# Modulation of a two-part sequence model: the weighted sum over input features is taken by VectorE, TensorE sums over partitions for three chunks at a time

## The chip, the cores and the metric

The kernel runs on one core of one Trainium2 chip. The metric is device time in microseconds of one execution of the whole program. Lower is better.

## The reference, cut to what matters

Two blocks of two layers each run one after the other on a sequence of 256 tokens with 1024 features. The first block mixes attention and a long convolution; its layers project the normed input with one wide matrix `w_in`. The second block's four sublayers are modulated by a vector that depends only on the conditioning input `c` (one row of 1024), not on the tokens:

```
def adaln(c, w, b):
    m = jax.nn.silu(c.astype(jnp.float32)) @ w + b
    shift, scale, gate = jnp.split(m, 3, axis=-1)
    return shift[:, None, :], scale[:, None, :], gate[:, None, :]
```

There are four such products, each of a 1 x 1024 row with a 1024 x 3072 matrix: 12288 outputs, each a sum over 1024 inputs. Since nothing but `c` goes in, the kernel computes all four while the first block runs. Everything is float32.

## The kernel before, in words

**Layout.** The four matrices are cut into 24 chunks of 512 output columns, 12 chunks for each layer `l` (0, 1) of the first block. A chunk is 2 MB: 128 partitions, and on each 8 slices of 512 numbers (input feature = slice k and partition). The projection weights of a layer are 16 chunks of the same size, named HV, Q, K_, V, HX1, HX2, ZA, ZH, GA0, GA1, GH0, GH1, PA, PH, WO0, WO1 (0 to 15).

**Loads.** `LOADS` is the order of the loads of a layer: w0 to w3, then m0, w4, m1, w5, ... m11, w15, where w is a projection chunk and m a modulation chunk. They go into a ring of four slots of `arena`. SyncE's queue (L406) issues them strictly in that order: load n waits until load n-4, which had the slot, is used up. `LOAD_END` says which TensorE group that is.

**Groups.** The program of a layer is the list `STEPS`, written out by hand in `layer_steps()`; every engine goes through it in order and does its share of each step. "proj" steps are TensorE groups of matmuls (two for each chunk up to GH1, four for PA and PH; WO0 and WO1 alternate for two token tiles). In this text g0 to g35 are the proj groups of a layer in order: chunk c has g2c and g2c+1 up to c = 11, PA is g24 to g27, PH g28 to g31, WO g32 to g35. Between the groups stand the attention and convolution steps of `after`: scores, mix (softmax weights), weigh, values, dft, idft, heads_out, heads_turn and so on.

**Two banks.** All groups, modulation groups too, write PSUM banks 0 and 1 in turn: group number `n` (`GROUP`, which numbers proj and modmul steps together) takes bank `n % 2`, and TensorE waits before it on `free[n % 2]`, that is until group n-2 has been drained. Q, K_, V, ZA to GH1 are drained by ScalarE, HX1, HX2, PA, PH by VectorE, WO by both.

**Modulation.** Before the first group of each chunk c from 4 on stands ("modmul", c-4): eight matmuls with 32 stationary columns (L592) on the eight slices of the chunk. `band` holds silu(c), one column of eight slices, with zeros around it, so that only row m of 32 gets chunk m's result, and the four column groups of the array each take two slices. ScalarE copies the bank out (L1272), and GpSimd adds it to `modsum` (L2311). Near the end of a layer ("mod", L599) turns the sums with four small matmuls.

**Chains.** On VectorE `link(ins)` lets the next instruction wait for this one.

## Time and profile before

| what | value |
|---|---|
| median of 3 runs | 1980.88 us (1980.46 to 1988.24) |
| span of the profiled execution | 1980.0 us |
| TensorE matmul busy in it | 1919.8 us, 97% |
| VectorE, ScalarE, GpSimd busy | 689.7, 372.2, 115.0 us |
| first block's layers in that profile | about 13.5 to 311 us, and 315 to 611 us |

The profiled execution has no time of its own beside its span on the page; the span lies 0.9 us under the median, so a difference read from the trace is a difference of the median. Times of rows are microseconds from the start of the span. In the groups of rows PE is TensorE's matmuls, DVE is VectorE, ACT ScalarE, POOL GpSimd, SPq SyncE's queue. One float32 matmul of the program shows as two matmuls in the profile.

### The profile page before, as it was taken

The numbers are of one execution on the slowest core, as the hardware profiler recorded it, in microseconds if no ns is written. First come the engines' busy times: TensorE is split into PE (matmuls) and PEld (weight loads), VectorE is DVE, ScalarE is ACT, GpSimd is POOL, SyncE is SP. The second block draws the span as 40 slices with busy tenths as digits, with TensorE's granted clock in tenths as the row PEclk, the third lists the DMA queues.
The fourth block names the chain that finished last, engine by engine and source line by source line (L and its number), as shares of the span: only waits on it lengthen the run. The fifth ranks groups of instructions, "written<-read, shape, count | busy, mean of one in ns | idle before, by whom it ended". The sixth has DMA issues, their size and how long they took to land.

```text
span 1980.0 us, 28488 instructions
## 1 busy us (share of the span) xinstructions
PE 1919.8 (97%) x11940; PEld 1070.5 (54%) x11940; DVE 689.7 (35%) x1472; ACT 372.2 (19%) x776; POOL 115.0 (6%) x98
## 2 busy tenths in 40 slices
PE   7999999999998999999989988999999999999998
PEld 6577866577865765776756544232323233333332
DVE  3364414354413573434449943010101010101112
ACT  3322102222103232234320012010101010101011
POOL 0000010000010000000016620000000000000000
PEclk9999999999999999999999998999999999999999
DMA  9255574264673316533323135999989999999993
GB/s 359 94 218 208 222 296 170 95 245 182 243 290 128 128 43 246 191 159 128 127 106 126 45 149 202 365 378 376 374 374 375 374 369 382 366 379 364 389 368 143
DMA packets 44037, 483.98 MB, mean 244 GB/s; under 512 B 5108, under 2 KB 6772, under 8 KB 10328
## 3 DMA queue, kind: packets, MB, share of 16 engines
q1 hardware_dynamic: 39136, 471.73, 59.2%
q10 hardware_dynamic: 4248, 9.07, 1.3%
q0 software_dynamic: 576, 2.10, 0.3%
q8 instruction: 55, 0.90, 0.2%
q14 instruction: 22, 0.18, 0.0%
HBM read 479.07 MB, written 10.10 MB: 247 GB/s over the span
## 4 chain that ended last, share of the span: by engine, by line
PE 88%; DVE 6%; DMA 3%; issue 1%; ACT 1%; ACTq 1%; POOL 0%; DVEq 0%; SPq 0%
PE bank L921 20%; PE bank L579 14%; PE bank L951 12%; PE bank L874 8%; PE bank L886 4%; PE bank L738 3%; PE bank L571 3%; PE bank L564 3%; PE bank L744 3%; PE bank L592 2%; PE bank L1000 2%; DMA arena<-bias_rows 1%; PE bank L1095 1%; PE bank L560 1%; PE bank L1028 1%; PE bank L935 1%
## 5 line engine op out<-in xcount | busy, mean ns | idle before, releaser
L921 PE MATMUL bank<-arena 128*32 128x512 f32 x4096 | 457.3, 592 | 0.0
L579 PE MATMUL bank<-arena 128*128 128x256 f32 x1408 | 313.3, 382 | 0.0
L921 PEld LDWEIGHTS bank<-arena 128*32 128x32 f32 x4096 | 136.1, 110 | 300.3 <-issue 300.3
L579 PEld LDWEIGHTS bank<-arena 128*128 128x128 f32 x1408 | 265.5, 190 | 54.2 <-issue 15.8
L951 PE MATMUL bank<-arena 128*32 128x512 f32 x2112 | 238.2, 595 | 0.0
L2077 DVE TENSOR_TENSOR arena<-arena,bank 128x256 f32<-128x256 f32 x64 | 27.0, 421 | 562.1 <-ACT arena L1447 511.6
L874 PE MATMUL bank<-arena 128*128 128x256 f32 x704 | 153.7, 379 | 0.1
L874 PEld LDWEIGHTS bank<-arena 128*128 128x128 f32 x704 | 133.6, 190 | 21.8 <-issue 4.1
L951 PEld LDWEIGHTS bank<-arena 128*32 128x32 f32 x2112 | 62.9, 109 | 133.3 <-issue 132.7
L1447 ACT ACTIVATE arena<-bank 128x256 f32<-128x256 f32 x64 | 24.6, 385 | 517.5 <-PE bank L921 517.4
L2323 POOL TENSOR_TENSOR arena<-arena 128x512 f32<-128x512 f32 x64 | 81.3, 1270 | 293.4 <-DVE arena L2131 290.9
L886 PE MATMUL bank<-arena 128*128 128x512 f32 x176 | 77.2, 592 | 0.0
L564 PE MATMUL bank<-arena 128*128 128x512 f32 x128 | 56.4, 596 | 1.8 <-ACT arena L1272 1.8
L738 PE MATMUL bank<-arena 128*128 128x256 f32 x256 | 56.8, 381 | 0.0
L744 PE MATMUL bank<-arena 128*128 128x512 f32 x128 | 56.4, 596 | 0.2 <-DVE arena L1966 0.2
L571 PE MATMUL bank<-arena 128*128 128x256 f32 x256 | 56.3, 381 | 0.0
L886 PEld LDWEIGHTS bank<-arena 128*128 128x128 f32 x176 | 33.4, 190 | 37.8 <-issue 37.3
L571 PEld LDWEIGHTS bank<-arena 128*128 128x128 f32 x256 | 48.3, 190 | 9.8 <-issue 3.4
L738 PEld LDWEIGHTS bank<-arena 128*128 128x128 f32 x256 | 48.2, 190 | 7.6 <-issue 0.8
L2052 DVE TENSOR_TENSOR arena<-arena,bank 128x256 f32<-128x256 f32 x22 | 9.3, 421 | 117.0 <-ACT arena L1422 116.9
L2311 POOL TENSOR_TENSOR arena<-arena 128x512 f32<-128x512 f32 x22 | 27.9, 1269 | 352.9 <-ACT arena L1272 352.9
L2334 POOL DMA_INDIRECT arena<-slot_rows,itab x4 | 4.0, 991 | 746.4 <-DVE itab L2214 745.5
(446 smaller groups left out, 1894.4 us busy)
## 6 DMA issues: line engine op xcount, KB each, us to landing
arena<-in_wgu SPq DMA_DIRECT2D x88, 2048.0 KB, 10.2
arena<-in_w SPq DMA_DIRECT2D x46, 2048.0 KB, 8.1
arena<-in_wdn SPq DMA_DIRECT2D x88, 1024.0 KB, 9.6
arena<-in_modw SPq DMA_DIRECT2D x24, 2048.0 KB, 9.3
arena<-in_wf SPq DMA_DIRECT2D x11, 3072.0 KB, 10.4
arena<-in_flt_deltas ACTq DMA_DIRECT2D x2, 1024.0 KB, 11.7
slot_rows<-arena ACTq DMA_DIRECT2D x7, 192.0 KB, 3.5
cst<-in_consts SPq DMA_DIRECT2D x1, 1162.0 KB, 7.7
```

What stands on the lines that cost most here:

```text
L564: ins = mm(bank[b][:, :], mT[:, k, h * P:(h + 1) * P], w[:, k * 512:(k + 1) * 512], start=(k == 0), stop=(k == KT - 1))
L571: ins = mm(bank[b][:, j * S:(j + 1) * S], w[:, col:col + P], y_in[:, k, :], start=(k == 0), stop=(k == 3))
L579: ins = mm(bank[b][:, j * S:(j + 1) * S], w[:, col:col + P], hT[:, k, :], start=(k == 0), stop=(k == KT - 1))
L592: ins = mm(bank[n % 2][r, :], band[:, k, 31 - c:63 - c], ring[at % RING][:, k * 512:(k + 1) * 512], start=(k < 4), stop=(k >= 4), skip_gro ...
L738: ins = mm(bank[n % 2][:, j * S:(j + 1) * S], w[:, col:col + P], hT[:, k, :], start=(k == 0), stop=(k == KT - 1))
L744: ins = mm(bank[n % 2][:, :], lhs(k), w[:, k * 512:(k + 1) * 512], start=(k == 0), stop=(k == KT - 1))
L874: ins = mm(bank[4 + f][:, u * S:(u + 1) * S], w[:, col:col + P], hT[:, k, :], start=(k == 0), stop=(k == KT - 1))
L886: ins = mm(bank[2 * t + i][:, :], hid[:, d % 2, f, t * P:t * P + P], w[:, col:col + 512], start=(d == 0 and f == 0), stop=(d == FFC - 1 an ...
L921: ins = mm(bank[w % 2][32 * j:32 * j + 32, :], hTe[:, k, TOK * b:TOK * b + TOK], wslot[SLOT[c]][:, k, :], start=(k == 0), stop=(k == KT - ...
L951: return mm(bank[4 + n][32 * g:32 * g + 32, :], lhs, dslot[c % RING][:, f, n * 512:(n + 1) * 512], start=first, stop=last, skip_group_chec ...
L1000: ins = mm(bank[6 + j // 4][:, (j % 4) * SLOTS:(j % 4 + 1) * SLOTS], xn[:, t, j * P:(j + 1) * P], oneh[:, t, 64:64 + SLOTS], start=(t == 0 ...
L2323: ins = pool.tensor_tensor(cz[o % 4][:, n], zz[:, o % 2], tab[o][:, n, :].unsqueeze(1).broadcast_to([P, 2, S]), ALU.mult)
```

## The change

The eight slices of a modulation chunk are no longer multiplied on TensorE. VectorE forms sum over k of silu(c)[k, p] * w[p, k, :] in SBUF: one tensor_scalar and seven scalar_tensor_tensor of 128 x 512 for each chunk, in two halves of four instructions (`modulation(l, m, part)`), each half put ahead of VectorE's share of a certain projection group (`MOD_SCALE`). TensorE sums the 128 partitions of three such sums in one group of four 32-column matmuls (one column group for each chunk, a fourth with zero weights), so a layer has four modmul groups in place of twelve: before g13, g22, g26 and g34 (`MOD_AT`). VectorE, not ScalarE, drains these banks and adds them to `modsum`; GpSimd does nothing for it any more. A modulation chunk's ring slot is given up when VectorE has ended its second half (`mod_sum`), not when TensorE has.

```diff
-GROUPS_1 = 36 + MOD_CHUNKS
+MOD_SETS = 4
+MOD_OF = MOD_CHUNKS // MOD_SETS
+MOD_AT = {13: 0, 22: 1, 26: 2, 34: 3}
+GROUPS_1 = 36 + MOD_SETS
+MOD_SCALE = {("proj", m + 3 + (1 + p) // 2, (1 + p) % 2): (m, p) for m in range(9) for p in range(2)}
+MOD_SCALE.update({("proj", PA, 2): (9, 0), ("proj", PA, 3): (9, 1), ("proj", PH, 0): (10, 0), ("proj", PH, 1): (10, 1), ("proj", WO0, 0): (11, 0), ("proj", WO1, 0): (11, 1)})
...
-                    sp.wait_ge(sm["grp_ps"], l * GROUPS_1 + LOAD_END[n - RING])
+                    if LOADS[n - RING][0] == "w":
+                        sp.wait_ge(sm["grp_ps"], l * GROUPS_1 + LOAD_END[n - RING])
+                    else:
+                        sp.wait_ge(sm["mod_sum"], l * MOD_CHUNKS + LOAD_END[n - RING])
...
                         pe.wait_ge(free[n % 2], l * (GROUPS_1 // 2) + n // 2)
-                        if c == 0:
-                            pe.wait_ge(sm["c_ready"], 1)
-                        pe.wait_ge(landed[at % RING], l * (16 * LOADS_1 // RING) + 16 * (at // RING + 1))
-                        for k in range(KT):
-                            r = slice(32 * (k % 4), 32 * (k % 4) + 32)
-                            ins = mm(bank[n % 2][r, :], band[:, k, 31 - c:63 - c], ring[at % RING][:, k * 512:(k + 1) * 512],
-                                     start=(k < 4), stop=(k >= 4), skip_group_check=True)
+                        pe.wait_ge(sm["mod_sum"], l * MOD_CHUNKS + MOD_OF * (c + 1))
+                        for q in range(4):
+                            m = MOD_OF * c + min(q, MOD_OF - 1)
+                            col = C_BAND + (31 - m if q < MOD_OF else 32)
+                            ins = mm(bank[n % 2][32 * q:32 * q + 32, :], cst[:, col:col + 32], mod_sums[m],
+                                     start=True, stop=True, skip_group_check=True)
...
+                            act.wait_ge(sm["grp_ps"], l * GROUPS_1 + GROUP[("modmul", 2, 0)] + 1)
...
-                        F(modout[:, c % 2, :], bank[n % 2][:, :], ACT.Copy).then_inc(free[n % 2], 1)
...
+            def modulation(l, m, part):
+                at = PLACE[("m", m)]
+                if part == 0:
+                    dve.wait_ge(landed[at % RING], l * (16 * LOADS_1 // RING) + 16 * (at // RING + 1))
...
+                w = ring[at % RING].rearrange("p (k n) -> p k n", k=KT)
+                for k in range(4 * part, 4 * part + 4):
+                    if k == 0:
+                        ins = v.tensor_scalar(mod_sums[m], w[:, 0, :], silu_c[:, 0:1], None, ALU.mult)
+                    else:
+                        ins = v.scalar_tensor_tensor(mod_sums[m], w[:, k, :], silu_c[:, k:k + 1], mod_sums[m], ALU.mult, ALU.add)
+                    if k < KT - 1:
+                        link(ins)
+                    else:
+                        ins.then_inc(sm["mod_sum"], 1)
...
+                    if step in MOD_SCALE:
+                        modulation(l, *MOD_SCALE[step])
...
+                    elif name == "modmul":
+                        n = GROUP[step]
+                        dve.wait_ge(sm["grp_ps"], l * GROUPS_1 + n + 1)
+                        if c == 0:
+                            if l:
+                                dve.wait_ge(sm["mod_ps"], l)
+                            ins = v.tensor_copy(modsum, bank[n % 2][:, :])
+                        else:
+                            ins = v.tensor_tensor(modsum, modsum, bank[n % 2][:, :], ALU.add)
+                        ins.then_inc(free[n % 2], 1)
+                        out_of(l, step)
...
-            for n in range(DEPTH * MOD_CHUNKS):
-                g = GROUP[("modmul", n % MOD_CHUNKS, 0)]
-                pool.wait_ge(free[g % 2], n // MOD_CHUNKS * (GROUPS_1 // 2) + g // 2 + 1)
```

The order of the instructions moves at three places that matter below. The first is VectorE in layer 0 around the forward transform of the convolution (dft, whose last instruction before is L1673 and after is L1717), before:

```order
L1673 TENSOR_TENSOR arena<-arena 128x512 [waits dve_chain] x2
L1673 TENSOR_TENSOR arena<-arena 128x512 [waits spec_ready]
L1673 TENSOR_TENSOR arena<-arena 128x512 [waits dve_chain]
L1737 COPY arena<-bank 128x256 [waits va_ps,spec_ready]
L1713 TENSOR_TENSOR arena<-bank,arena 128x2x256 [waits sc_ps,va_used]
L1713 TENSOR_TENSOR arena<-bank,arena 128x2x256 [waits dve_chain]
L1715 TENSOR_REDUCE small<-arena 128x4 [waits dve_chain]
```

L1737 is the copy of attention values and L1713 begins the scores of head 3. In the changed kernel the same place reads:

```order
L1717 TENSOR_TENSOR arena<-arena 128x512 [waits dve_chain] x2
L1717 TENSOR_TENSOR arena<-arena 128x512 [waits spec_ready]
L1717 TENSOR_TENSOR arena<-arena 128x512 [waits dve_chain]
L1781 COPY arena<-bank 128x256 [waits va_ps,spec_ready]
L1622 COPY arena<-bank 128x512 [waits grp_ps,va_used]
L1584 TENSOR_SCALAR arena<-arena,ev 128x512 [waits fp_ps,landed2,odd_free]
L1586 SCALAR_TENSOR_TENSOR arena<-arena,ev 128x512 [waits dve_chain] x3
L1757 TENSOR_TENSOR arena<-bank,arena 128x2x256 [waits sc_ps,dve_chain]
```

L1622 is the drain of the first modmul group, L1584 and L1586 are a half of a modulation chunk. The drain stands behind the whole transform.

The second place is VectorE after the attention heads have been turned (L1763 before, L1807 after, is the gating of the heads); before, the second inverse transform (L1697, L1702, L1705 four times) and then the drains of PA (L1617):

```order
L1697 SCALAR_TENSOR_TENSOR arena<-arena,vec,bank 128x256 [waits dve_chain]
L1702 TENSOR_TENSOR arena<-arena 128x256 [waits dve_chain]
L1705 TENSOR_TENSOR arena<-arena 128x256 [waits dve_chain]
L1617 TENSOR_TENSOR arena<-bank,arena 128x512 [waits odd_free,grp_ps,even_free,z_ready]
L1617 TENSOR_TENSOR arena<-bank,arena 128x512 [waits grp_ps,odd_free]
```

After, from the end of the same inverse transform (L1741, L1746, L1749):

```order
L1741 SCALAR_TENSOR_TENSOR arena<-arena,vec,bank 128x256 [waits dve_chain]
L1746 TENSOR_TENSOR arena<-arena 128x256 [waits dve_chain]
L1749 TENSOR_TENSOR arena<-arena 128x256 [waits dve_chain]
L1586 SCALAR_TENSOR_TENSOR arena<-arena,ev 128x512 [waits z_ready]
L1586 SCALAR_TENSOR_TENSOR arena<-arena,ev 128x512 [waits dve_chain] x3
L1584 TENSOR_SCALAR arena<-arena,ev 128x512 [waits wg_ready,landed2]
L1586 SCALAR_TENSOR_TENSOR arena<-arena,ev 128x512 [waits dve_chain] x3
L1624 TENSOR_TENSOR arena<-arena,bank 128x512 [waits grp_ps,dve_chain]
```

L1624 is the drain of the second modmul group; two halves, and a third ahead of the inverse transform, now stand before it.

The third place is TensorE at the same time, from the turn of the heads (L711 before) on. Before, a modmul group (L592) stands before each chunk:

```order
L711 MATMUL bank<-cst,arena 128x128 x7
L592 MATMUL bank<-arena 32x512 [waits landed2,odd_free]
L592 MATMUL bank<-arena 32x512 x7
L579 MATMUL bank<-arena 128x256 [waits landed3,even_free]
L579 MATMUL bank<-arena 128x256 x15
L579 MATMUL bank<-arena 128x256 [waits odd_free]
L579 MATMUL bank<-arena 128x256 x15
L592 MATMUL bank<-arena 32x512 [waits landed0,even_free]
L592 MATMUL bank<-arena 32x512 x7
L571 MATMUL bank<-arena 128x256 [waits ya_ready,landed1,odd_free]
```

After (L720 is the turn, L600 a modmul group, L589 the groups of GH1, L581 the first of PA):

```order
L720 MATMUL bank<-cst,arena 128x128 x7
L600 MATMUL bank<-arena,cst 32x512 [waits mod_sum,odd_free]
L600 MATMUL bank<-arena,cst 32x512 x3
L589 MATMUL bank<-arena 128x256 [waits landed3,even_free]
L589 MATMUL bank<-arena 128x256 x15
L589 MATMUL bank<-arena 128x256 [waits odd_free]
L589 MATMUL bank<-arena 128x256 x15
L581 MATMUL bank<-arena 128x256 [waits ya_ready,landed1,even_free]
```

The modmul group is half as long and the one before PA is gone. The second group of GH1 takes the bank of the modmul group in both programs; in the changed one it is VectorE that has to free it.

## Rows read from the trace of the kernel before

**Rows 1.** The page: engine busy times and the chain that ended last

```profile
PE 1919.8 (97%) x11940; PEld 1070.5 (54%) x11940; DVE 689.7 (35%) x1472; ACT 372.2 (19%) x776; POOL 115.0 (6%) x98
...
PE 88%; DVE 6%; DMA 3%; issue 1%; ACT 1%; ACTq 1%; POOL 0%; DVEq 0%; SPq 0%
```

**Rows 2.** Chain that ended last, second layer: start, length, what

```profile
420.71 1.72 PE bank L664 x4
422.43 0.89 PE bank L704 x8
423.32 6.91 PE bank L579 x32
430.23 0.44 PE bank L695 x4
430.66 1.06 PE bank L685 x8
431.73 1.85 PE bank L592 x16
...
433.59 7.17 PE bank L579 x32
```

**Rows 3.** Timeline of VectorE, second layer: start, length, line, instruction

```profile
403.30 0.54 DVE L1597 TENSOR_SCALAR arena<-bank,vec 128x256 f32<-128x256 f32 x1 [6.00 <-PE bank L579]
...
406.53 0.18 DVE L1720 RECIPROCAL small<-small 128x4 f32<-128x4 f32 x1
...
408.43 0.48 DVE L1729 SCALAR_TENSOR_TENSOR arena<-arena,small 128x256 f32<-128x256 f32 x1
...
413.51 1.42 DVE L1713 TENSOR_TENSOR arena<-bank,arena 128x512 f32<-128x512 f32 x2
...
416.22 0.17 DVE L1716 TENSOR_SCALAR small<-small 128x4 f32<-128x4 f32 x1
...
442.62 0.69 DVE L1665 TENSOR_TENSOR arena<-bank,arena 128x512 f32<-128x512 f32 x1 [0.17 <-PE bank L664]
...
455.67 0.42 DVE L1737 COPY arena<-bank 128x256 f32<-128x256 f32 x1
```

**Rows 4.** The same view, later: heads, second inverse transform, drains, norm

```profile
529.69 2.04 DVE L1763 SCALAR_TENSOR_TENSOR arena<-bank,small,arena 128x256 f32<-128x256 f32 x4 [16.82 <-PE bank L711]
531.77 0.48 DVE L1697 SCALAR_TENSOR_TENSOR arena<-arena,vec,bank 128x256 f32<-128x256 f32 x1
...
532.75 1.44 DVE L1705 TENSOR_TENSOR arena<-arena 128x256 f32<-128x256 f32 x1
...
538.07 0.42 DVE L1705 TENSOR_TENSOR arena<-arena 128x256 f32<-128x256 f32 x1
...
578.41 0.69 DVE L1620 TENSOR_TENSOR arena<-arena 128x512 f32<-128x512 f32 x1
...
612.75 1.41 DVE L1783 SCALAR_TENSOR_TENSOR arena<-arena,small 128x512 f32<-128x512 f32 x2
...
616.13 0.88 DVE L1546 TENSOR_SCALAR arena<-arena,small 128x512 f32<-128x512 f32 x2
```

**Rows 5.** Timeline of TensorE, four places: in brackets idle before, releaser

```profile
315.28 3.68 PE L516 MATMUL bank<-cst,arena 128*128 128x128 f32 x16 [4.31 <-DVE arena L1539]
318.77 8.06 PE L579 MATMUL bank<-arena 128*128 128x256 f32 x32
...
580.35 7.10 PE L564 MATMUL bank<-arena 128*128 128x512 f32 x16 [0.92 <-ACT arena L1272]
...
778.73 1.94 PE L516 MATMUL bank<-cst,arena 128*128 128x128 f32 x16 [0.94 <-DVE arena L1539]
```

**Rows 6.** Busy time by stretch; before DMA share and GB/s stands the granted clock

```profile
315.20:317.00 1.80, 1.72 (x8) 1.72 (x9) 1.07 (x4) 0.40 (x3) 0.00 (x0) 0.50 1.00 428
```

**Rows 7.** The ring's loads: L406's landing times, and the DMA rate of a stretch

```profile
DMA to landing us min/median/max: 7.3/8.8/16.6
...
266.00:272.00 6.00, 6.00 (x30) 5.28 (x29) 2.60 (x4) 0.00 (x0) 0.00 (x0) 1.00 1.02 431
```

More of the change, by code:

```diff
@@ L48 @@
     0, 128, 256, 384, 896, 1408, 1920, 2432, 2688, 2690, 2708, 3220, 3284)
-C_UP, C_LM, C_S4 = 3285, 3413, 3605
-C_N = 3637
+C_UP, C_LM, C_S4, C_BAND = 3285, 3413, 3605, 3637
+C_N = 3701
 HV, Q, K_, V, HX1, HX2, ZA, ZH, GA0, GA1, GH0, GH1, PA, PH, WO0, WO1 = range(16)
@@ L94, in layer_steps @@
     for n, step in enumerate(g):
-        c, h = step[1:]
-        if c >= 4 and h == 0:
-            m = c - 4
-            out.append(("modmul", m, 0))
+        if n in MOD_AT:
+            out.append(("modmul", MOD_AT[n], 0))
         if step == g[-1]:
@@ L111 @@
 YSQ = {GROUP[("proj", WO0 + i, t)]: 2 * t + i + 1 for t in range(TT) for i in range(2)}
-LOAD_END = [max(n for (name, c, _), n in GROUP.items() if name == {"w": "proj", "m": "modmul"}[kind] and c == chunk) + 1
+LOAD_END = [max(n for (name, c, _), n in GROUP.items() if name == "proj" and c == chunk) + 1 if kind == "w" else chunk + 1
             for kind, chunk in LOADS]
@@ L261, in model @@
         modsum = view(att + 4096, 512)
-        band = view(att + 4608, KT, 63)
-        modout = view(att + 5120, 2, 512)
+        early_sums = [view(at, 512) for at in (att + 4608, att + 5120)]
+        mod_sums = early_sums + [view(at, 512) for at in (big1 + 3072, big1 + 3584)] + early_sums\
+            + [view(at, 512) for at in (att, att + 512)] + early_sums + [view(at, 512) for at in (att + 2048, att + 2560)]
+        silu_c = ev[:, E_C:E_C + KT]
         biasr = view(LOW + 3072, 4, TT, S)
@@ L357, in model @@
                 on_ready yt_ps ya_ready
[L358 removed]
+                macc_used mod_ps mod_sum mask_landed gb_in gb_ps gb_ready
                 gla_ps gla_act gla_in gla_done cl_ready fsc_ps fsc_ready fpr_ready fw_ready ft_ps fpt_ready fva_ps
@@ L584, in _ @@
                         n = GROUP[step]
-                        at = PLACE[("m", c)]
                         pe.wait_ge(free[n % 2], l * (GROUPS_1 // 2) + n // 2)
-                        if c == 0:
-                            pe.wait_ge(sm["c_ready"], 1)
-                        pe.wait_ge(landed[at % RING], l * (16 * LOADS_1 // RING) + 16 * (at // RING + 1))
-                        for k in range(KT):
-                            r = slice(32 * (k % 4), 32 * (k % 4) + 32)
-                            ins = mm(bank[n % 2][r, :], band[:, k, 31 - c:63 - c], ring[at % RING][:, k * 512:(k + 1) * 512],
-                                     start=(k < 4), stop=(k >= 4), skip_group_check=True)
+                        pe.wait_ge(sm["mod_sum"], l * MOD_CHUNKS + MOD_OF * (c + 1))
[4 more added lines that the diff above has]
+                                     start=True, stop=True, skip_group_check=True)
                         ins.then_inc(sm["grp_ps"], 1)
                     elif name == "mod":
-                        pe.wait_ge(sm["mod_in"], (l + 1) * MOD_CHUNKS)
+                        n = GROUP[("modmul", MOD_SETS - 1, 0)]
+                        pe.wait_ge(free[n % 2], l * (GROUPS_1 // 2) + n // 2 + 1)
                         for j in range(4):
@@ L1266, in _ @@
                         ins.then_inc(free[n % 2], 1)
-                    elif name == "modmul":
-                        n = GROUP[step]
-                        act.wait_ge(sm["grp_ps"], l * GROUPS_1 + n + 1)
-                        if l * MOD_CHUNKS + c >= 2:
-                            act.wait_ge(sm["mod_in"], l * MOD_CHUNKS + c - 1)
-                        F(modout[:, c % 2, :], bank[n % 2][:, :], ACT.Copy).then_inc(free[n % 2], 1)
                     elif name == "mod":
@@ L1558, in norm @@
                 dve.wait_ge(sm["ht_ready"], 4 * n + 4)
+            def modulation(l, m, part):
+                at = PLACE[("m", m)]
+                if part == 0:
+                    dve.wait_ge(landed[at % RING], l * (16 * LOADS_1 // RING) + 16 * (at // RING + 1))
+                    if l + m == 0:
+                        dve.wait_ge(sm["c_ready"], 1)
+                    if m == 0 and l:
+                        dve.wait_ge(sm["grp_ps"], l * GROUPS_1)
+                    elif m in (2, 3):
+                        dve.wait_ge(sm["fp_ps"], l * 8 + 8)
+                    elif m in (4, 5, 8, 9):
+                        dve.wait_ge(sm["grp_ps"], l * GROUPS_1 + GROUP[("modmul", (m - 4) // MOD_OF, 0)] + 1)
+                    elif m in (6, 7):
+                        dve.wait_ge(sm["wg_ready"], l * 4 + 4)
+                    elif m >= 10:
+                        dve.wait_ge(sm["yt_ps"], l * 2 + 2)
+                w = ring[at % RING].rearrange("p (k n) -> p k n", k=KT)
[8 more added lines that the diff above has]
+                        ins.then_inc(sm["mod_sum"], 1)
             link(v.memset(small[:, :], 0.0))
-            link(v.memset(band.rearrange("p a b -> p (a b)"), 0.0))
             v.memset(small[:, 95:96], 1e-6).then_inc(sm["x_ready"], 1)
```

13 lines of the change are left out of this document (2 added, 11 removed).

## The prediction

> **What bounds the kernel now.** I read the page first: TensorE is busy 97% of the span and makes up 88% of the chain that ended last, VectorE is busy 35% [rows 1]. So what leaves TensorE's queue is time won, as long as nothing that TensorE waits for gets later. The chain inside a layer confirms it: one TensorE piece follows the next, and a modulation group is a piece of 1.85 us among them [rows 2]. Then I read the timelines of VectorE and TensorE over the second layer step by step, since the change gives VectorE work at fixed places of an in-order program. The first layer repeats the pattern from its g7 on, so everything below is worked out for one layer and doubled. The clock and the loads are read last [rows 6, 7].
>
> **What is removed.** Twelve modulation groups a layer at 1.85 us are 22.2 us. Ahead of WO0 TensorE also waited 0.92 us for ScalarE to drain the last of them [rows 5], and the changed program has no modulation group there. Together 23.1 us a layer. ScalarE's and GpSimd's shares were off the chain.
>
> **What is added on TensorE.** Four groups of four such matmuls instead of eight. The eight used the four column groups of the array twice; four use them once, so half of 1.85: 0.93 us, or 3.7 us a layer. Bounds: from that half up to the full 1.85, which would be 7.4.
>
> **What is added on VectorE.** The nearest scalar_tensor_tensor with both tensors in SBUF takes 1.41 us for two of 128 x 512 [rows 4], 0.69 us and some 0.03 to the next, so 0.72. The nearest tensor_scalar takes 0.44 [rows 4]. A first half is 0.44 + 3 x 0.72 = 2.65 us, a second half 2.9 us, a chunk 5.5 us, a layer 67 us. Over the layer VectorE has idle time enough, but not everywhere. In one thing it gets lighter: two instructions took 1 us more while GpSimd's adds ran, as the 1.44 us of an L1705 beside the usual 0.42 shows [rows 4]; I take that out below.
>
> **First hold: the bank behind the transform.** The first modmul group stands before g13 and takes bank 1; g14 takes bank 1 again and needs VectorE's drain, which stands behind the whole dft step. Follow both engines from the end of g8 (403.25 in this trace).
> VectorE has no pause from there on. Drains of g8 to g11, 3.2 us each (403.30 to 406.53), 12.8; three mixes of 2.4 (406.53 to 408.91), 7.2; two scores of 2.9 (413.51 to 416.39), 5.8; two copies, 0.9; the transform 13.05 (442.62 to 455.67) [rows 3]; two modulation chunks, 11.1; the drain itself 0.7, like other 128 x 512 operations on PSUM [rows 3]. Sum 51.6 us, bank free about 51.7 after g8.
> TensorE from the same point: g9 to g13 at 6.9 to 7.2 us, 35.2; three times weigh and scores, 0.44 + 1.06, 4.5; twice transform and values, 1.72 + 0.89, 5.2 [rows 2]; the modmul group 0.9. Sum 45.8 us. TensorE waits **5.9 us** for the bank. Before, ScalarE drained these banks, and no such wait is in the chain.
>
> **Second hold.** The second modmul group follows heads_turn directly, before g22, and g23 needs its bank. VectorE can start on the heads only when they are turned, and then does: the heads 2.1; half a chunk 2.65; the inverse transform 5.7 (531.77 to 538.49 is 6.7, less the 1.0 of GpSimd); a second half 2.9; a first half 2.65; the drain 0.7 [rows 4]. Sum 16.8. TensorE has 0.9 for the modmul group and 7.0 for g22 [rows 2]. It waits **8.9 us**.
>
> **Smaller waits.** WO0 needs the last drain of PH, two operations of 0.69 [rows 4] and their gaps: 1.5 us, now without a modulation group in front. g34 needs g33 drained by ScalarE and then VectorE, two operations of 128 x 512 on a bank one after the other at about 0.7 each [rows 3] and two hand-overs, some 1.7 us, of which the fourth modmul group covers 0.9: 0.8 us. The third modmul group stands among PA groups of 3.5 us, and VectorE drains it at once: nothing.
>
> **The clock.** After TensorE had been idle 4.31 us before a norm, its transposes took 3.68 us, against 1.94 us for the same sixteen after an idle of 0.94 [rows 5]; the next group took 8.06 us against 7.17 [rows 5, 2]. The granted clock of the stretch was 0.50, the lower level of 1.2 GHz [rows 6]. That is 1.74 + 0.89 = 2.6 us lost behind the wait. Both holds are longer than 4.31 us. I charge 2.5 us behind each, with 0 and 2.6 as bounds.
> The Trainium skill says the same in TensorE: Matmul & The Clock Gate, What's actually happening: "the default state is throttled, and activity releases the throttle". By this rule both holds are charged, and without it the sum would be 5.0 us a layer lower; the trace agrees at its norms.
>
> **The loads.** A modulation chunk's slot is now given up by VectorE. After the second hold's queue, m8 can be issued only when m6 is used up, 2.1 + 2.65 + 5.7 + 2.9 = 13.4 us after the heads are turned, and w12 (PA's weights, whose own slot was long free) stands behind it in the queue. A load alone lands after 7.3 us, and a second one behind it needs some 5.0 more (2.1 MB at 431 GB/s are 4.9) [rows 7]; so w12 lands 25.7 us after heads_turn. TensorE comes to PA at 16.8 + 7.0 = 23.8, or with the slow clock at 26.3. So either the clock costs 2.5 us here or the load 1.9, not both. After that the queue holds m9, w13, the norm's gains, m10 and ScalarE's loads for the next layer within some 30 us; by this arithmetic each lands about when it is needed, with 1 to 3 us to spare.
>
> **Sum.** One layer: -23.1 + 3.7 + 5.9 + 8.9 + 1.5 + 0.8 + 2.5 + 2.5 = **+2.7 us**. Two layers: +5.4 us. The span would be 1985, and since the median lay 0.9 above it, the median 1986.
>
> **Rivals.**
> *A, the holds without the clock.* If the clock does not fall, w12's landing costs 1.9 instead: -23.1 + 3.7 + 5.9 + 8.9 + 1.5 + 0.8 + 1.9 = -0.4 a layer, 1980. For it: a free-standing wait in a layer is not a norm. Against it: the rows show the fall at half the idle time of the second hold.
> *B, loads late behind VectorE.* If the DMA rate near PA and PH falls, because two queues share it or m8 and w12 move together, m8 and m10 arrive 2 to 5 us late, and because a half of a chunk stands before the drain of a PA or PH group, VectorE holds the bank and TensorE waits. Landing times of up to 16.6 us [rows 7] speak for it, the 1 to 3 us to spare against. It costs 3 to 8 us a layer more: 1992 to 2001. It counts as slower from 2.3 us a layer on.
> The Trainium skill has a rule for this in DMA: Bandwidth & Descriptors, Issuing engines are not separate DMA queues: transfers run on the same 16 engines whoever issues them. By it ScalarE's loads take from SyncE's; no row at this place shows it yet.
> *C, the change does what it says.* The holds would have to vanish: with only 3.7, 1.5 and 0.8 added, -17.1 a layer, 1947. Even if the operations of a chunk took half the time (1.4 us less for each half), the first hold falls to 0.3 and the second to 4.7 with its clock, -9.2 a layer or 1962. The 0.69 us for an SBUF-only operation [rows 4] speaks against both. It counts as faster by the bound below from 7.6 us a layer less waiting than I sum up.
>
> **Chances and range.** Forecast 0.48, A 0.2, B 0.25, C with 1947 or 1962 0.07. Measurement tells no change from one of 0.5%, 9.9 us, so the bounds are 1971 and 1990.8. The forecast's own range is 1981 to 1991 (a hold off by 1 us each, modmul groups dearer by up to 0.9, clock 1.5 to 2.6); of its 0.48 some 0.03 lies above the bound. Faster 0.07, within 0.5% 0.65, slower 0.28. Range 1976 to 1997: below lies C, above the upper part of B.
>
> **What would show it.** Right: in each layer a TensorE idle of some 6 us before g14 and of some 9 us before g23, both released by VectorE's drain (L1622, L1624), with a granted clock of 0.5 behind; VectorE without pause from g8 to the drain; VectorE busy more by 24 chunks of 5.5 us, 133 us, less what GpSimd's adds cost it. Wrong: a scalar_tensor_tensor of the chunk well off 0.69 us, a modmul group off 0.93, a wait for w12 or w13 at PA or PH, or a pause of VectorE on a landing.

## The result, and the profile after

The changed kernel takes 1996.9 us in the median of 4 runs (1990.5 to 2001.7), beside 1982.6 for the kernel before, timed with it: a ratio of 1.006, 95% interval 1.0033 to 1.0087. Run again later (below), it gave 1993.7 against 1981.5, ratio 1.005 (1.0034 to 1.0067). So it is slower by 0.3 to 0.9%, at the edge of what I had said a measurement can tell from no change. The forecast was 1986.0, 5.1 us over the kernel before; 12 to 14 us were measured. That is past the 9.9 us from which I would call it slower, an outcome to which I had given 0.28. The profiled execution (1990.5, span 1988.6) was the quickest of the four.

The page of the kernel after, busy times and chain, against [rows 1]:

```profile
PE 1891.5 (95%) x11620; PEld 1066.4 (54%) x11620; DVE 824.4 (41%) x1671; ACT 358.8 (18%) x752; POOL 85.9 (4%) x74
...
PE 78%; DVE 14%; DMA 5%; issue 2%; ACT 1%; ACTq 1%; POOL 0%; DVEq 0%; SPq 0%
```

TensorE lost 28 us of busy time, and its part of the chain fell from 88% to 78%: VectorE's went up from 6% to 14%. A share of TensorE that falls while the span grows is the sign of waits. Here they are, in the timeline of TensorE, second layer (in brackets the idle time ahead and its releaser):

```profile
441.53 1.06 PE L600 MATMUL bank<-arena,cst 128*32 128x512 f32 x8
442.57 7.17 PE L589 MATMUL bank<-arena 128*128 128x256 f32 x32
...
457.68 8.89 PE L589 MATMUL bank<-arena 128*128 128x256 f32 x32 [6.44 <-DVE arena L1622]
...
546.71 8.75 PE L589 MATMUL bank<-arena 128*128 128x256 f32 x32 [8.94 <-DVE arena L1624]
555.65 7.14 PE L581 MATMUL bank<-arena 128*128 128x256 f32 x32 [0.20 <-issue]
562.73 1.06 PE L600 MATMUL bank<-arena,cst 128*32 128x512 f32 x8
563.73 14.08 PE L581 MATMUL bank<-arena 128*128 128x256 f32 x64
578.32 3.72 PE L581 MATMUL bank<-arena 128*128 128x256 f32 x16 [0.51 <-DVE arena L1664]
582.79 3.72 PE L581 MATMUL bank<-arena 128*128 128x256 f32 x16 [0.75 <-DVE arena L1664]
588.29 13.97 PE L574 MATMUL bank<-arena 128*128 128x512 f32 x32 [1.78 <-DVE arena L1664]
602.20 1.07 PE L600 MATMUL bank<-arena,cst 128*32 128x512 f32 x8
603.83 7.13 PE L574 MATMUL bank<-arena 128*128 128x512 f32 x16 [0.57 <-DVE arena L1820]
```

The four L600 rows are the modulation groups. The holds are at g14 (457.68) and g23 (546.71), each released by a drain on VectorE. A drain takes 0.69 us; what counts is what stands in front of it. VectorE's timeline of the kernel after, ahead of both drains (L1622 at 456.94, L1624 at 545.97):

```profile
443.41 0.69 DVE L1709 TENSOR_TENSOR arena<-bank,arena 128x512 f32<-128x512 f32 x1
...
453.57 2.87 DVE L1717 TENSOR_TENSOR arena<-arena 128x512 f32<-128x512 f32 x4
456.48 0.43 DVE L1781 COPY arena<-bank 128x256 f32<-128x256 f32 x1
456.94 0.69 DVE L1622 COPY arena<-bank 128x512 f32<-128x512 f32 x1
...
529.36 2.04 DVE L1807 SCALAR_TENSOR_TENSOR arena<-bank,small,arena 128x256 f32<-128x256 f32 x4 [9.72 <-PE bank L720]
531.44 0.49 DVE L1584 TENSOR_SCALAR arena<-arena,ev 128x512 f32<-128x512 f32 x1
531.97 2.33 DVE L1586 SCALAR_TENSOR_TENSOR arena<-arena,ev 128x512 f32<-128x512 f32 x3
534.33 0.48 DVE L1741 SCALAR_TENSOR_TENSOR arena<-arena,vec,bank 128x256 f32<-128x256 f32 x1
...
540.06 3.11 DVE L1586 SCALAR_TENSOR_TENSOR arena<-arena,ev 128x512 f32<-128x512 f32 x4
543.09 0.48 DVE L1584 TENSOR_SCALAR arena<-arena,ev 128x512 f32<-128x512 f32 x1
543.61 2.33 DVE L1586 SCALAR_TENSOR_TENSOR arena<-arena,ev 128x512 f32<-128x512 f32 x3
545.97 0.69 DVE L1624 TENSOR_TENSOR arena<-arena,bank 128x512 f32<-128x512 f32 x1
```

TensorE's group for the first drain was done at 442.6, a microsecond before VectorE began the 13 us of the transform. Note the 9.72 us in which VectorE stood idle just before the second hold.

The granted clock (third number from the end) right behind each hold, and the modulation's operation:

```profile
457.68:460.00 2.32, 2.32 (x6) 1.87 (x7) 2.21 (x4) 0.00 (x0) 0.00 (x0) 0.50 0.00 0
...
546.71:550.00 3.29, 3.29 (x8) 2.66 (x9) 2.99 (x4) 0.00 (x0) 0.00 (x0) 0.51 1.02 438
...
L1586 DVE SCALAR_TENSOR_TENSOR arena<-arena,ev 128x512 f32<-128x512 f32 x168 | 126.3, 752 | 5.7
```

0.50 is the lower level, 1.2 GHz. g14 took 8.89 us instead of 7.17. The first layer has the same two holds (6.44 and 8.94 us), and behind the second one more wait than the second layer's 0.20:

```profile
253.29 7.14 PE L581 MATMUL bank<-arena 128*128 128x256 f32 x32 [1.62 <-issue]
```

From one norm's transposes to the next norm's, the second layer took 300.80 us before (315.28 to 616.08) and 304.49 after (319.31 to 623.80): +3.7. I compare the runs below by this layer time too, because it leaves out the start and the rest of the program, where executions of one and the same kernel differ. Each layer time is that of one trace, and the kernel after, traced twice, gave 304.5 and 305.4: differences under 1 us are not read.

### The profile page after: what moved, and what is told of

It is laid out like the page before. It is cut to its first block, busy times and chain, and to the rows that moved or that the text cites. A ratio compares the mean times of both kernels' runs of the same rounds, so it can differ in the third digit from the quotient of the medians.

```text
span 1988.6 us, 27961 instructions
## 1 busy us (share of the span) xinstructions
PE 1891.5 (95%) x11620; PEld 1066.4 (54%) x11620; DVE 824.4 (41%) x1671; ACT 358.8 (18%) x752; POOL 85.9 (4%) x74
## 4 chain that ended last, share of the span: by engine, by line
PE 78%; DVE 14%; DMA 5%; issue 2%; ACT 1%; ACTq 1%; POOL 0%; DVEq 0%; SPq 0%
PE bank L930 20%; PE bank L960 12%; PE bank L589 9%; PE bank L883 8%; PE bank L895 4%; PE bank L747 3%; PE bank L574 3%; PE bank L753 3%; DVE arena L1586 3%; DMA arena<-in_modw 2%; PE bank L1009 2%; DMA arena<-bias_rows 1%; PE bank L1104 1%; PE bank L570 1%; PE bank L1037 1%
## 5 line engine op out<-in xcount | busy, mean ns | idle before, releaser
L930 PE MATMUL bank<-arena 128*32 128x512 f32 x4096 | 457.5, 592 | 0.4 <-issue 0.4
L589 PE MATMUL bank<-arena 128*128 128x256 f32 x1408 | 320.8, 388 | 30.8 <-DVE arena L1624 17.9
L589 PEld LDWEIGHTS bank<-arena 128*128 128x128 f32 x1408 | 270.9, 194 | 81.2 <-DVE arena L1624 18.7
L930 PEld LDWEIGHTS bank<-arena 128*32 128x32 f32 x4096 | 136.1, 110 | 301.6 <-issue 301.6
L883 PE MATMUL bank<-arena 128*128 128x256 f32 x704 | 153.7, 379 | 0.1
L1586 DVE SCALAR_TENSOR_TENSOR arena<-arena,ev 128x512 f32<-128x512 f32 x168 | 126.3, 752 | 5.7
L2356 POOL TENSOR_TENSOR arena<-arena 128x512 f32<-128x512 f32 x64 | 81.3, 1271 | 293.4 <-DVE arena L2175 290.8
L581 PE MATMUL bank<-arena 128*128 128x256 f32 x256 | 57.1, 382 | 3.2 <-issue 1.8
L747 PE MATMUL bank<-arena 128*128 128x256 f32 x256 | 56.8, 381 | 0.0
L581 PEld LDWEIGHTS bank<-arena 128*128 128x128 f32 x256 | 48.1, 190 | 13.1 <-DVE arena L1664 2.6
L1087 PE MATMUL bank<-arena 32*128 32x256 f32 x128 | 37.3, 421 | 9.7 <-DVE arena L2175 8.9
```

The costliest lines, as they stand in the source:

```text
L581: ins = mm(bank[b][:, j * S:(j + 1) * S], w[:, col:col + P], y_in[:, k, :], start=(k == 0), stop=(k == 3))
L589: ins = mm(bank[b][:, j * S:(j + 1) * S], w[:, col:col + P], hT[:, k, :], start=(k == 0), stop=(k == KT - 1))
L747: ins = mm(bank[n % 2][:, j * S:(j + 1) * S], w[:, col:col + P], hT[:, k, :], start=(k == 0), stop=(k == KT - 1))
L883: ins = mm(bank[4 + f][:, u * S:(u + 1) * S], w[:, col:col + P], hT[:, k, :], start=(k == 0), stop=(k == KT - 1))
L930: ins = mm(bank[w % 2][32 * j:32 * j + 32, :], hTe[:, k, TOK * b:TOK * b + TOK], wslot[SLOT[c]][:, k, :], start=(k == 0), stop=(k == KT - ...
L1586: ins = v.scalar_tensor_tensor(mod_sums[m], w[:, k, :], silu_c[:, k:k + 1], mod_sums[m], ALU.mult, ALU.add)
```

## The experiments

Two theories to begin with. Mine: the work saved on TensorE is real, and it is given back by where the drains and the chunk halves stand in VectorE's program. The rival: VectorE has too much to do, so that its lateness comes back at the next wait wherever things are put. Median, ratio to before with its interval, and second layer of all runs:

| run | median us | ratio (95%) | second layer us |
|---|---|---|---|
| before, first trace; e12_before | 1980.9; 1984.9 | 1.001 (0.9995, 1.0025) | 300.8; 301.0 |
| after; e9_after | 1996.9; 1993.7 | 1.006; 1.005 | 304.5; 305.4 |
| e1_first | 1991.3 | 1.0033 (1.0020, 1.0045) | 301.5 |
| e2_drain | 1993.4 | 1.0045 (1.0032, 1.0059) | 305.0 |
| e3_swap | 1984.7 (1983.3 without one execution of 8714) | 1.0009 (0.9992, 1.0026) | 301.9 |
| e5_busy | 1986.5 | 1.0013 (1.0002, 1.0023) | 301.0 |
| e4_early | 1970.2 | 0.9928 (0.9901, 0.9954) | 292.8 |
| e6_both | 1964.7 | 0.9898 (0.9869, 0.9926) | 289.4 |
| e7_both | 1948.6 | 0.9827 (0.9797, 0.9856) | 284.5 |
| e8_less | (2077.7) | see there | 297.4 |
| e10_drain0 | 1984.2 | 1.0012 (0.9993, 1.0031) | 300.3 |
| e11_all | 1959.9 | 0.9868 (0.9828, 0.9908) | 287.5 |

### e1_first: the first modulation group two groups later

```
-MOD_AT = {13: 0, 22: 1, 26: 2, 34: 3}
+MOD_AT = {15: 0, 22: 1, 26: 2, 34: 3}
```

> Edit: the changed kernel with its first modmul group before g15 instead of g13, so that VectorE's drain of it no longer stands behind the transform. Theory 1 (holds of the bank by VectorE's order): the idle of 6.4 us before g14 and the 1.8 us of slow clock behind it vanish; TensorE then catches up with VectorE's backlog at the second transposition (turn 1), which costs 0.8 us; so 7.4 us a layer, about 15 us off the changed kernel's profiled span of 1988.6, giving 1974. Rival (VectorE's extra 134 us bound the stretch whatever the order): the wait moves to weigh or turn and the span stays within 4 us of 1988.6.

A miss: 1991.3. g14 is free of its hold, but the next group with a bank to wait for is not. TensorE and ScalarE of e1_first:

```profile
461.13 1.07 PE L600 MATMUL bank<-arena,cst 128*32 128x512 f32 x8
466.75 8.80 PE L589 MATMUL bank<-arena 128*128 128x256 f32 x32 [4.55 <-ACT arena L1270]
...
462.28 0.51 ACT L1314 ACTIVATE arena<-arena,small 128x256 f32<-128x256 f32 x1 [11.78 <-DVE small L1760]
...
464.80 1.28 ACT L1270 ACT_TABLE_LOAD   x1
466.10 0.60 ACT L1270 ACTIVATE arena<-bank 128x512 f32<-128x512 f32 x1
```

ScalarE could have drained g14 at 456.7. But ahead of it in ScalarE's order stands the exp of scores 3 (L1314), which waited 11.78 us for VectorE. VectorE's lateness reached TensorE by way of a third engine. The second layer gained 3.0 us, where 1974 asked for some 7; the rival's "within 4 us of 1988.6" fits the median.

### e2_drain: the second drain right behind the heads

At its old place, not shown, the drain is skipped.

```
 v.scalar_tensor_tensor(yaT[:, j, :], ...)          # end of the heads
+dve.wait_ge(sm["grp_ps"], l * GROUPS_1 + n + 1)    # n = GROUP[("modmul", 1, 0)]
+v.tensor_tensor(modsum, modsum, bank[n % 2][:, :], ALU.add).then_inc(free[n % 2], 1)
```

> Edit: the changed kernel with VectorE's drain of the second modmul group moved ahead of everything but the gating of the heads. The idle of 8.9 us before g23 must go in both theories. Theory 1 with the load queue: m8 is still issued only when m6 is used up, 14.1 us after the heads are turned, with PA's weights w12 behind it, so w12 lands some 26 us after heads_turn and TensorE, which now is at PA after 15, waits some 11 us for w12: the span stays within 3 us of 1988.6. Rival (only the bank held TensorE): 10.7 us a layer less, 1967.

Held. g23 starts at once, and PA waits 11.72 us, more than the 8.94 that g23 did (TensorE of e2_drain):

```profile
534.65 13.76 PE L589 MATMUL bank<-arena 128*128 128x256 f32 x63
560.13 8.96 PE L581 MATMUL bank<-arena 128*128 128x256 f32 x32 [11.72 <-issue]
```

Two waits lay over each other: the bank, and PA's weights w12, which stand in SyncE's order behind chunk 8, which waits for VectorE to use up chunk 6. Mending one alone is worth nothing: the layer takes 305.0 us, against 304.5.

### e3_swap: e2, with w12 asked for ahead of chunk 8

```
-for n in range(RING, LOADS_1 + RING):
+for n in [*range(RING, PLACE[("m", 8)]), PLACE[("w", PA)], PLACE[("m", 8)], *range(PLACE[("m", 9)], LOADS_1 + RING)]:
```

> Edit: as the run with the drain moved, and SyncE issues w12 ahead of m8. Theory 1: no wait on w12 at PA any more; VectorE is then late with m8's second half (27.8 us after heads_turn), so the third modmul group, due at 23, waits some 6 us; against the changed kernel 4 to 5 us a layer less, 1979. Rival (only the load mattered): 10 us a layer less, 1968. Rival (VectorE's work bounds the stretch): no gain over the run with the drain alone.

The mechanism held, with 6.80 us at the third modulation group for the 6 expected. The gain was smaller than expected: the layer is 2.6 us shorter than that of the kernel after, not 4 to 5, and the median lies at 1983 to 1985 where 1979 was expected. "No gain over e2" is out, with 3.2 us a layer. The row of e3_swap:

```profile
554.11 1.94 PE L600 MATMUL bank<-arena,cst 128*32 128x512 f32 x8 [6.80 <-DVE arena L1663]
```

VectorE waited 1.92 us for chunk 8 to land and worked at its eight slices until 553.4; drains of two PA groups (L1663) stood behind it. This is a third wait below the other two. It costs less than they did, and the kernel is back at the time of before (ratio 1.0009, with 1 in its interval).

### e5_busy: TensorE kept at work in the holds

```
+if (c, h) in ((ZH, 0), (GH1, 1)):
+    if c == ZH:
+        pe.wait_ge(sm["wt_ready"], l * 4 + 3)
+    for _ in range(6 if c == ZH else 9):
+        mm(bank[6 if c == ZH else 4][:, :], ident, cst[:, C_FC:C_FC + 512], start=True, stop=True)
```

> Edit: the changed kernel with useless matmuls in the two holds (six of 128 x 512 before g14 into bank 6, nine before g23 into bank 4, about 5.2 and 7.7 us), whose results nobody reads. Theory 1 (the clock term): the idle shrinks to about 1.2 us each, the granted clock stays 1.00 in g14 and g23, which take 7.1 and 7.0 us instead of 8.9 and 8.8; 3.5 us a layer less, less what w12's landing takes back behind g23 (some 1.5), so 2 to 3.5 us a layer, 1982 to 1985, and the runs scatter less than the 11 us of the changed kernel if the clock is what scatters. Rival (clock falls by the waiting itself or by power): no change, 1988, and clock 0.5 behind the holds.

Idle before g14 and g23 is 1.09 and 1.22 us now, and both groups take 7.17 with the clock at its upper level (e5_busy, third number from the end of the last two rows):

```profile
458.27 7.17 PE L594 MATMUL bank<-arena 128*128 128x256 f32 x32 [1.09 <-DVE arena L1627]
...
545.58 7.17 PE L594 MATMUL bank<-arena 128*128 128x256 f32 x32 [1.22 <-DVE arena L1629]
...
458.27:465.44 7.17, 7.17 (x34) 6.34 (x35) 6.89 (x10) 1.32 (x5) 0.00 (x0) 1.00 0.01 2
545.58:552.70 7.12, 7.12 (x32) 5.99 (x32) 5.77 (x9) 0.00 (x0) 0.00 (x0) 1.00 1.00 430
```

So the slow clock costs 1.7 us at g14 (8.89 - 7.17) and 1.6 at g23 (8.75 - 7.17). The layer is 3.5 us shorter than that of the kernel after (301.0 against 304.5), but not by these two terms alone: TensorE's wait for w12 came back with 1.97 us, the waits at PH fell from 1.3 to 0.5, and 0.9 us were won before g14 already, where this execution lost less behind the norm. The median, 1986.5, lies 1.5 above my range, with runs from 1982.3 to 1991.9: the scatter did not get less, as I had thought it would.

### e4_early and e6_both: halves into VectorE's idle time

```
 ins.then_inc(sm["on_ready"], 1)              # heads are out, VectorE waits for them turned
+for m, part in ((6, 0), (6, 1), (7, 0)):
+    modulation(l, m, part)
```

> The drain of the second modulation group stands right behind the heads, as in e2, and three halves (both of chunk 6 and the first of chunk 7) are worked before VectorE waits for the turned heads, in a stretch in which it stood idle for 9.7 us. Theory (what costs time is where the halves stand in VectorE's order, and the idle stretches would hold them): no hold at g23, so the 8.9 us and the 1.75 us of clock go; chunk 8 and w12 are asked for sooner, so the 11.7 us that TensorE waited for w12 in e2 and the 6.8 us of the third modulation group in e3 shrink to under 2 us together; the first hold of 6.4 us stays. By the terms of a layer that leaves -23.1 + 3.8 + 6.4 + 1.8 + some 4 us of small waits, -7.3 a layer, and a median of 1983.7 - 14.6 = about 1967 (1962 to 1974). Rival (VectorE has too much to do in this stretch, so that the time returns at the next wait, as in e1): the second layer ends where that of e3 does (last WO group at 604.5 us) and the median is that of e3, 1985, within 3.

> e4_early with the first modulation group two projection groups later, as in e1. e1 showed that this only moves the first hold to the next group (4.55 instead of 6.4 us idle, the same 1.8 us of clock), since ScalarE's drain stands behind the exp of scores 3. So against e4_early a gain of about 2 us a layer: a median 4 us below that of e4_early (2 to 6). Rival (with the later part free of holds the first one is worth its whole 8.2 us): 15 us below e4_early.

e4_early also takes these three halves out of `MOD_SCALE` and moves the second drain as e2 does; e6_both adds e1's place for the first modulation group, 15.

Both as the theory says. e4_early has neither the hold of g23 nor a wait for w12 nor one at the third modulation group; its layer is 11.7 us shorter than that of the kernel after. The rival is out for this stretch: VectorE had the time, in the wrong place. e6_both lies 5.5 below e4_early (4 expected), with e1's hold still there.

### e7_both: e4, and the first stretch in another order

```
+MOD_AT = {16: 0, 22: 1, 26: 2, 34: 3}
+MOD_SCALE.update({("proj", ZH, 1): (3, 0), ("weigh", 3, 0): (3, 1), ("turn", 1, 0): (4, 0)})
```

> e4_early with the first modulation group three projection groups later (behind g15), and both halves of chunk 3 behind the second inverse transform's values instead of around scores 3, where VectorE is late. Theory (e1's hold at g15 was ScalarE's exp of scores 3, which waited for VectorE): scores 3 come 5.7 us sooner counting both halves' places, so ScalarE drains g14 in time, no group of the first stretch is held over 1 us, the clock stays at 1.00 there, and the gain over e4_early is 6.4 + 1.8 = about 8 us a layer: a median some 16 us below e4_early, about 1950. Rival (VectorE's backlog from the first transform is too long whatever the order): a hold of 3 to 5 us stays at g15 or g16, with its clock, and the median is that of e6_both within 3.

Not shown: e4's three halves and moved drain are in it too.

1948.6 where 1950 was expected. g14 starts without a wait at 429.16. TensorE of e7_both from g15 on, which e1 had held, to g16, and the granted clock over it:

```profile
440.68 7.07 PE L595 MATMUL bank<-arena 128*128 128x256 f32 x32
447.59 0.60 PE L710 MATMUL bank<-cst,arena 128*128 128x128 f32 x4
448.03 1.13 PE L669 MATMUL bank<-cst,arena 128*128 128x128 f32 x8
449.09 1.07 PE L606 MATMUL bank<-arena,cst 128*32 128x512 f32 x8
450.09 7.17 PE L595 MATMUL bank<-arena 128*128 128x256 f32 x32
...
440.00:470.00 30.00, 30.00 (x148) 24.42 (x147) 22.72 (x40) 9.01 (x17) 0.00 (x0) 1.00 0.49 202
```

TensorE is busy for all 30 us. This kernel beats both, before by 1.7% (1.4 to 2.0), with the same arithmetic as the kernel after: only places in three orders differ.

### e8_less: two slices a half instead of four

```
-for k in range(4 * part, 4 * part + 4):
+for k in (0, 1) if part == 0 else (4, KT - 1):
```

> The kernel after with its order untouched, but every half of a chunk adds up two slices instead of four (slices 0, 1, 4 and 7; the others are left out of the modulation), so that VectorE works some 1.5 us less in each half and waits and loads stay as they are. Theory (the holds are VectorE's halves ahead of its two drains: 5 halves lie ahead of the first, some 5 ahead of the second): g14 is held 0 to 1 us, g23 at most 2, the clock stays at 1.00 in both, and the median falls by 2 x (6.4 + 8.9 + 1.8 + 1.75) or nearly so, to 1955 to 1965. Rival (the holds are the transfers or the order of the waits, not VectorE's working time): both holds stay over 4 us and the median within 5 of 1996.

The median says nothing here: this kernel leaves half of the slices out of the modulation, and the later part of the program then does more work (4608 matmuls of L930 for 4096; 1460.7 us from the second layer's end, 1364 to 1371 in all other runs), which I had not thought of. The layer can be read: 297.4 us, and the two holds in TensorE's timeline of e8_less:

```profile
454.80 9.35 PE L589 MATMUL bank<-arena 128*128 128x256 f32 x32 [4.67 <-DVE arena L1622]
...
539.57 9.63 PE L589 MATMUL bank<-arena 128*128 128x256 f32 x32 [4.22 <-DVE arena L1624]
```

My theory's numbers (0 to 1 us, and at most 2) failed, and both holds stay over 4 us, as the rival had it; but they do shrink, so VectorE's working time is a part of them. g14's hold falls by 1.8 us only, although four halves with two operations of 0.79 less, 6.3 us, lie between g8 and the transform. VectorE now has pauses of 1.0, 2.2 and 1.1 us there, so most of the time saved is gone before the transform begins. My reading is that g14's hold is 13 us of transform in front of a ready drain first, and halves second; e10_drain0 below tests it. g23's falls by 4.7, which is three halves of 1.57 less: between the heads and that drain VectorE has no pause in either kernel.

### e10_drain0 and e11_all: the first drain ahead of the transform

```
+if c == 0:                                   # at the head of VectorE's dft step
+    v.tensor_copy(modsum, bank[n % 2][:, :]).then_inc(free[n % 2], 1)
```

> The kernel after with one drain moved: VectorE copies the first modulation group out of its bank directly ahead of the first forward transform instead of behind it (TensorE has that group's sums at 442.6 us of the profiled execution, VectorE starts the transform at 443). No half is moved. Theory, after the run with two slices a half (what holds g14 is above all the transform's 13 us ahead of the drain, not the halves): g14 starts as soon as scores 3 are issued, the 6.4 us and 1.8 us of clock go, and since g15's bank is g13's here, which ScalarE emptied before the exp of scores 3, the hold doesn't come back at g15; the late exp of scores 3 shows at g16 or at weigh 3 with at most 1 us. Median 16 us below e9_after, about 1980. Rival (the backlog of VectorE is due anyway, as in e1): a hold of 3 to 5 us at weigh 3 or g16, with its clock, and only 4 to 5 us below e9_after.

> e4_early and e10_drain0 together: both drains right behind the step at which their groups are ready, three halves in the idle stretch, MOD_AT as in the kernel after. Theory: the two stretches add up, so the median is 16 below e4_early, 1954, within 5 of e7_both (1948.6), with no idle of TensorE over 1 us between the first scores and PH. Rival (e7_both also gained from having chunk 3's halves out of the way of scores 3): 5 to 10 us above e7_both, with a hold left at g15 to g17 or at weigh 3.

e10_drain0 is 9.6 us below e9_after, between the 16 of the theory and the 4 to 5 of the rival. g14 starts at once and g15 too, but VectorE's inverse transform is late for the turn behind g15 (TensorE of e10_drain0):

```profile
468.44 1.23 PE L663 MATMUL bank<-cst,arena 128*128 128x128 f32 x8 [2.47 <-DVE arena L1755]
469.50 8.76 PE L589 MATMUL bank<-arena 128*128 128x256 f32 x32
```

2.47 us, and 1.6 of clock in g16 (8.76 against 7.17) remain of 6.44 and 1.7: 4.1 of 8.1 us won, as the layer has it (300.3 against 304.5). With e4's edit, e11_all is 5.3 us a layer below e4_early and 3.0 above e7_both; its median, 1959.9, misses the theory's 1954 and is 11.3 above e7_both, past the rival's 5 to 10. It still has the 2.47 us at the turn and 1.6 of clock in g16, which e7_both has not. Chunk 3's two halves stand in front of that turn here and not in e7_both, but e7_both also moves a half of chunk 4 and the modulation group, so which of these moves is worth how much is not shown. So in the first stretch the rival is half right: order alone moves the drain, but VectorE's backlog has to be cleared too.

### e9_after and e12_before: the two kernels once more

> The kernel after, unchanged, beside the others of this call. Its four runs so far lie between 1990.5 and 2001.7, so the same program is timed again on the chip on which the variants run: expected within 1990 to 1997, with the second layer's last WO group ending at 618 to 619 us as before, and whatever more it takes lying behind the two layers.

> The kernel before, unchanged, profiled once more. Its times spread over 10 us, like those of the kernel after. Over the traces of the kernel after and its variants three parts can be told apart: the start (TensorE waits 0.3 to 3.9 us for the rows of the bias, with up to 3 us of clock behind it), the two layers, and the rest (1363.9 to 1371.4 us from the second layer's end). If the spread has nothing to do with the change, this trace has a second layer of 300.8 us within 0.5 (from one norm's transposes to the next), and a start or a rest that differs from that of the first trace of before by up to some microseconds. If the layer itself varies by 1 us or more, the layer times of single traces can't be compared as finely as I compare them.

e9_after's last WO group ended at 626.3, 7.5 us later than I expected, and not in the layers alone. At the start it waited for the bias rows, three times as long as the first trace of the kernel after (1.26), and at a lower clock behind it. Of its 7.1 us over that trace 5.5 lie ahead of the first attention piece (L641, at 56.57 and 51.04 us) and 2.0 in the two layers. And e12_before waited at 1087.8 for weights of a later stage, where the first trace of before has 0.30 us. The row of e9_after, and that of e12_before:

```profile
49.11 6.77 PE L617 MATMUL bank<-arena,cst 128*128 128x512 f32 x8 [3.94 <-DMA arena<-bias_rows]
```

```profile
1087.81 6.26 PE L1042 MATMUL bank<-arena 128*128 128x256 f32 x16 [2.44 <-DMA arena<-in_w]
...
1087.81:1094.07 6.26, 6.26 (x17) 4.82 (x17) 4.30 (x8) 0.42 (x1) 4.61 (x4) 0.58 0.47 202
```

Over the traces with the full modulation this second wait is 0.3 to 0.8 or 2.3 to 2.6 us long. The kernel before met it both ways, the kernel after short both times (0.30 and 0.38), its variants either way. The rest of the program, from the second layer's end to the span's, takes 1363.9 to 1364.9 us in all runs with the short wait but one (e6_both, 0.80 and 1369.5), and 1368.2 to 1371.4 in those with the long one. The start scatters from none to 3.9 us of wait with 0 to 3 us of clock (6.77 us for a piece that takes 3.80 at full speed). Layer times are steady within 1 us: 300.8 and 301.0 before, 304.5 and 305.4 after.

## Why the prediction was right, and where it was off

The median lies 0.1 us inside the stated range of 1976 to 1997 and outside the forecast's own 1981 to 1991. The direction and the terms inside a layer were foreseen; that the median still fell inside the range is luck.

**Removed and added on TensorE.** Four modulation groups at 1.06, 0.95 of it to the next piece: 3.8 us for 3.7.

**The holds.** 6.4 for 5.9, and 8.9 for 8.9. Undoing each showed the mechanism: e2 and e10 moved one drain each and their holds went. The chunk operations, priced at 0.72, took 0.75 (0.79 to the next).

**The clock.** It fell behind both holds. Here the size was off: 1.7 and 1.6 us for 2.5 each in the kernel after, and 1.5 to 2.9 over both layers of the other runs (8.63 to 10.02 us for 7.17). The 2.6 was one norm's, and I took it as nearly fixed. e5 confirmed the mechanism and the size. The Trainium skill's rule in TensorE: Matmul & The Clock Gate, What's actually happening, that activity releases the throttle, is borne out: matmuls whose results nobody reads, put into the two waits, kept the granted clock at 1.00.

**The smaller waits.** WO0 1.8 for 1.5, g34 0.6 for 0.8. Not foreseen, 1.3 in the second layer: the two waits of 0.5 and 0.75 at PH, each behind a half of chunk 10 that VectorE works before the drain. That is rival B's mechanism at less than half its price; chunk 10 was 17.1 us in landing, and VectorE stood idle 1.97 us for it. In the first layer these waits are only 0.2.

**The loads.** w12 landed 26.3 us after the heads were turned, for 25.7, and TensorE waited 0.2 for it in the second layer: there "either the clock or the load, not both" holds, and e5 shows the other side, where the clock is saved and 1.97 us of wait for w12 return. The first layer has both, 1.6 us of clock and 1.62 of wait, so the "not both" holds in one layer of two; e9_after has 2.0 and 1.43 there.

**The sum.** -23.1 + 3.8 + 6.4 + 8.9 + 1.7 + 1.6 + 0.2 + 1.3 + 1.8 + 0.6 = +3.2 us, the layer has +3.7 (e9_after +4.6), and +2.7 was forecast. So a clock that was priced too high hid PH's waits in the second layer, and PH's and w12's together in the first.

**The step that failed** is the last one, from span to median. The spans of the two first traces differ by 8.6 us, for 5.4 forecast: 3.8 in the first layer (from the first attention piece to the second norm), 3.7 in the second, 0.2 ahead of them and 0.9 behind them. For e9_after it is 15.7: 4.9, 4.6, 5.7 at the start and 0.4 behind. So the two layers are 7.5 to 9.5 us, and the medians differ by 12 to 14. I added one trace's 0.9 us, as if a difference of two traces were one of the medians. It is not: a timed execution is 1.9 us longer than its span (1990.5 for 1988.6), so the first trace of after lies 6.4 us under its median and that of before 0.7. Over all traces the rest of the program differs by up to 7.5 us, mostly with the length of one wait for a load of a later stage, and the start by up to 6 (the first attention piece begins at 50.7 to 56.6 us). Both traces of the kernel after have the short wait at that load, so it explains neither of them; a slow start explains e9_after. What the untraced executions of the kernel after had, and whether slow starts or long waits are more frequent with it, stays open. The median came out where rival B was placed, but not for B's reason: B's waits are 1.3 of its 3 to 8 us a layer.

**Two slips of arithmetic** change nothing: C's terms add up to -9.6 a layer, not -9.2 (still 1962), and B's upper end is 2002, not 2001.

**Rival C** was argued with one wrong number. I said that with operations of half the time the first hold falls to 0.3; e8 measured 4.67. My sum ran from g8 "without pause", which is true of the loaded VectorE, not of a lighter one.

## What to carry to other kernels

Work moved to an engine with 65% idle time can still cost TensorE its full time where a drain stands behind it: three lighter halves took 4.7 us off the second hold, all of what they saved, but four took only 1.8 of 6.3 off the first, where VectorE had pauses to lose them in. So ask of each bank who frees it, how long that instruction has been ready, and what stands between, and look for an earlier place for the drain: one drain ahead of a 13 us transform gave 4 us a layer back, and three halves moved into a wait, with the second drain, 12. Expect waits in layers: bank, weights and next drain lay over each other here, and taking away the top one alone changed nothing. Follow lateness across engines too, since a third engine's in-order queue passes it on.

## What the runs showed of the hardware

What one fall of TensorE's clock costs in a layer did not go by the length of the wait. It was 1.6 us behind an idle time of 4.55 us (e1) and behind one of 2.47 (e10), 1.7 behind 6.4 and 1.6 behind 8.9 in the kernel after, but 1.9 behind the same 6.4 in e9_after, and 2.2 and 2.5 behind 4.7 and 4.2 in e8. In first layers it was up to 2.5 (e9_after, behind 6.45) and 2.9 (e8, behind 4.66). At the start, waits of 2.3 and 3.5 us for the bias cost 1.7 each (5.49 and 5.48 us for 3.80), those of 3.0 (e4_early) and 3.9 cost 3.0, and e12_before's of 2.23 nothing. The waits of up to 1.8 us in the kernel after cost no clock (two WO groups behind 1.78 us took 13.97), but in the first 22 us of e6_both and e11_all a group behind a wait of 1.23 and 1.15 us took 8.86. So two waits of 2.5 us can cost more clock than one of 9, by these rows 3.2 us against 1.6.

A wait for a load that was 2 us longer went with 5.6 us more behind the second layer (1363.9 against 1369.5 us for before). What is lost there is clock, not the wait: the group behind it took 6.26 us at a granted clock of 0.58, where the first trace has 3.69. The group starts at about the same time in both executions, 470.1 and 470.9 us behind the end of the second layer (468.5 to 471.5 in all traces with the full modulation), since the first trace had lost as much just before it to a slow clock (two pieces of 2.07 and 3.63 us for 1.13 and 1.92). By TensorE's next wait 3.4 of the 5.6 us are there. The other 2.2 come later and stay open: no experiment was made on that stretch. And e6_both has the long rest (1369.5) with the short wait, so this wait is not shown to be the whole cause.
